# Hybrid decoder layer: one inverse form kept on TensorE and ScalarE, layer norms scaled in tile pairs

## The chip, the cores and the metric

The kernel runs on 1 core of one Trainium2 chip. The metric is device time in microseconds (us). A core has TensorE (PE: matmul; its weight loads are shown apart as PEld), VectorE (DVE), ScalarE (ACT), GpSimd (POOL) and SyncE (SP, here only DMA issues). Each runs its own list of instructions in order and waits on semaphores.

## The reference

One layer of a decoder for a prompt of 512 tokens and 8 decoding rows, width 1024. Eight heads do windowed attention, eight heads RWKV-7 time mixing; then an output projection, a layer norm, a gated convolutional FFN and a second layer norm.

```python
def layer_norm(x, g, b):
    xf = x.astype(jnp.float32)
    mu = jnp.mean(xf, -1, keepdims=True)
    xc = xf - mu
    var = jnp.mean(xc * xc, -1, keepdims=True)
    return (xc * lax.rsqrt(var + LN_EPS) * g + b).astype(x.dtype)

    # rwkv7_time_mix
    def step(S, inp):
        r_t, w_t, k_t, v_t, kk_t, a_t = inp
        sa = jnp.einsum('bhvk,bhk->bhv', S, -kk_t)
        S = S * w_t[:, :, None, :] + sa[..., None] * (kk_t * a_t)[:, :, None, :] + v_t[..., None] * k_t[:, :, None, :]
        return S, jnp.einsum('bhvk,bhk->bhv', S, r_t)

    # decoder_layer
    x1 = layer_norm(ALPHA * x + h, ln1_g, ln1_b)
    f, conv_T = conv_ffn(x1, conv_prev, w_ffn_in, conv_w, conv_b, w_ffn_out)
    y = layer_norm(ALPHA * x1 + f, ln2_g, ln2_b)
```

The recurrence over the prompt is computed in chunks of 64 tokens. For a chunk, the products of sa with each other form a unit lower triangular system, whose 64x64 inverse is needed for each head.

## The kernel before

The order of every engine is written out by hand, and semaphores count what is done. `own` behind an instruction makes an engine wait for its own result.

Stages by time: input projection with attention beside it (to about 222 us), the chunk recurrence (222 to 357), output projection with the group norm beside it (to 450), first layer norm beside the first FFN tiles (to 474), FFN (to about 836), second layer norm beside and behind the last tile of the down projection.

**The inverse.** The prompt is 4 blocks (n) of 128 tokens, each of two chunks j, held on partitions 0-63 and 64-127. `xx` holds the growing inverse X in two forms for all 8 heads: form 0 (transposed, on the other chunk's partitions) and form 1. Five levels (l = 1 to 5) double the solved size, from pairs to 64. In each level, for two groups g of 4 heads:

- `half_products` (PE): a 64x64 product of the system `lower` with form 0 for each head and chunk, into banks[4g], columns 0 to 255.
- `halves` (VectorE): that result times the mask `level[l]`, 128x256, into `lower[.., 1]`. Both groups come before any update.
- `full_products` (PE): its product with form 1 of X, in both forms, 16 products of 64x64 for a group (8 in the last level), columns 256 to 511 of banks[4g] and banks[4g+1].
- `update` (VectorE): X minus the result, both forms in one 128x512 operation; the last level makes only `xf`.

fp32 products show two matmul records each. The 64x64 products use one quarter of the array each, given by the partitions of input and output. The rest of the recurrence is laid between the levels: on PE, behind the half products of a level, the key scores (l = 1), value scores (l = 2, 3) and step terms (l = 3); in level 1 `value_side` and in level 2 `solved` are interleaved with the half products; behind the full products of level 4 come the chain product and the value terms of the block before. VectorE masks the key and value scores between `halves` and `update`, makes the transitions in level 4, and sums decode scores.

**First layer norm.** z holds 8 tiles of 128 channels, 520 tokens in two halves of 260. Per half: sums on PE, mean on VectorE, spread over partitions by a product, `ln_centre` in pairs of tiles, `ln_square` (ScalarE), sums, `ln_root` (ScalarE), `ln_recip` (VectorE), spread into bank 5. Then `ln_scale` (VectorE) multiplies tile by tile with the gain and the spread value, and `ln_shift` (ScalarE) adds the bias twice per tile: into `x1_hi`, rounded, and into z. The low part z - x1_hi is made by VectorE for pairs 0 and 2 (`even_low`), by POOL for pairs 1 and 3 (`odd_low`). PE's `ffn_half` (tile i of the FFN, one half of the tokens) waits before each k pair for its low part, for i = 0. `second_mean`, `second_var` and `second_spread` place the products of half 1's norm inside `ffn_half(0..2, 0)`, after the named k tile. `ffn_half(0, 1)` is the first that needs half 1.

**Second layer norm.** The mean of the first 7 tiles is taken off early; the last tile's down projection runs half by half. Then `l2_last`, `l2_stats`, `l2_root`, `l2_recip`, `l2_centre` (pairs), `l2_scale` (tiles) and `l2_shift` (ScalarE, the bias) lead to four stores `y_out` for each half.

## Time and profile before

| | |
|---|---|
| median of 3 runs | 873.22 us (870.77 to 873.72) |
| profiled execution | 872.92 us, span 871.1 us |
| mean granted TensorE clock | 0.984 |
| PE busy | 815.2 us, 94% |
| VectorE busy | 494.8 us, 57% |
| ScalarE busy | 330.9 us, 38% |
| POOL busy | 274.0 us, 31% |

The span goes from the first to the last instruction; the profiled execution's own time is 1.8 us longer. Times in timelines are us from the start of the span. In a timeline row stand the start, the duration (of the whole run where "xN" is over 1), engine, line, operation, output and inputs, and in brackets the idle time before it and what ended it. Many operations share the lines of helpers (L1241, L1244, L1850), so tiles tell them apart.

### The profile page before, as it was taken

The page shows a single profiled execution, that of the slowest core. Times are in us where ns is not written, and L with a number is a line of the kernel's source. Part 1 is how long each engine was busy: PE and PEld are TensorE (multiplying, and loading weights), DVE is VectorE, ACT ScalarE, POOL GpSimd, SP SyncE. Part 2 cuts the span into 40 slices and gives each one's busy share as a digit, 9 for nine tenths or more (in the row PEclk, how much of TensorE's full clock was granted, in tenths as well). Part 3 has the DMA queues.
Part 4 walks back from the last instruction along what each step waited for, and adds up shares of the span by engine and source line. Part 5 has one row for each costly group of instructions (what it writes and reads, how often), then busy time and mean ns, then how long its engine had stood idle before and what let it go on. Part 6 is the DMA issues. An engine that isn't in the chain of part 4 may idle for free.

```text
span 871.1 us, 23141 instructions
## 1 busy us (share of the span) xinstructions
PE 815.2 (94%) x10012; PEld 763.6 (88%) x10012; DVE 494.8 (57%) x764; ACT 330.9 (38%) x569; POOL 274.0 (31%) x121
## 2 busy tenths in 40 slices
PE   6999999999887777899998999999999999999994
PEld 6899889898677676688888999999999999999994
DVE  5588766786577666265354777766667661000037
ACT  5644565454313122433265434333333331111124
POOL 0000000000297670325252444444344434344300
PEclk9999999999999999999998999999999999999997
DMA  7232133152243343703111333223322332333202
GB/s 267 84 97 74 49 98 98 49 198 61 88 116 107 107 126 118 237 15 104 58 54 44 98 113 106 80 91 98 97 86 85 98 88 89 92 88 89 85 2 99
DMA packets 32470, 83.47 MB, mean 96 GB/s; under 512 B 5144, under 2 KB 10456, under 8 KB 31728
## 3 DMA queue, kind: packets, MB, share of 16 engines
q1 hardware_dynamic: 32368, 81.98, 30.7%
q8 instruction: 79, 1.29, 0.6%
q14 instruction: 23, 0.19, 0.1%
HBM read 75.87 MB, written 5.91 MB: 94 GB/s over the span
## 4 chain that ended last, share of the span: by engine, by line
PE 86%; DVE 7%; ACT 3%; issue 2%; POOL 1%; DMA 0%; DVEq 0%; ACTq 0%; POOLq 0%
PE banks L1850 83%; PE banks L1904 1%; DVE z L1241 1%; DVE xx L1241 1%; PE banks L2253 1%; DVE ms L1241 1%; DVE rw L1241 1%; DVE z L1244 1%; POOL wr_lo L697 1%; DVE ssa L1505 1%; ACT x_hi L1149 0%; ACT z L1152 0%; ACT z L1212 0%; DMA w_raw<-in_w 0%; ACT nv L982 0%
## 5 line engine op out<-in xcount | busy, mean ns | idle before, releaser
L1850 PE MATMUL banks<-x_hi,w_hi 128*128 128x264 f32 (+1 forms) x784 | 207.7, 298 | 11.4 <-DVE x_lo L1241 8.9
L1850 PE MATMUL banks<-x_hi,w_lo 128*128 128x264 f32 (+1 forms) x784 | 198.3, 286 | 0.0
L1850 PE MATMUL banks<-x_lo,w_hi 128*128 128x264 f32 (+1 forms) x784 | 198.3, 286 | 0.0
L1850 PEld LDWEIGHTS banks<-x_hi,w_hi 128*128 128x128 f32 x784 | 138.9, 191 | 24.5 <-issue 11.3
L1850 PEld LDWEIGHTS banks<-x_lo,w_hi 128*128 128x128 f32 x784 | 139.1, 192 | 0.1
L1850 PEld LDWEIGHTS banks<-x_hi,w_lo 128*128 128x128 f32 x784 | 138.9, 191 | 0.0
L697 POOL TENSOR_TENSOR w_lo<-w_raw,w_hi 128x1024 fp32r<-128x1024 f32 (+1 forms) x38 | 90.6, 2385 | 152.2 <-ACT w_hi L825 152.0
L697 POOL TENSOR_TENSOR wx_lo<-w_raw,wx_hi 128x1024 fp32r<-128x1024 f32 (+1 forms) x34 | 81.8, 2406 | 100.5 <-ACT wx_hi L825 100.1
L1244 DVE SCALAR_TENSOR_TENSOR z<-z,banks 128x260 f32<-128x260 f32 (+1 forms) x24 | 12.4, 515 | 122.1 <-PE banks L1850 121.9
L1850 PE MATMUL banks<-x_hi,wx_lo 128*128 128x260 f32 x352 | 73.5, 283 | 0.0
L1850 PE MATMUL banks<-x_hi,wx_hi 128*128 128x260 f32 x352 | 73.5, 282 | 0.0
L1850 PE MATMUL banks<-x_lo,wx_hi 128*128 128x260 f32 x352 | 73.4, 283 | 0.0
L706 POOL MEMSET kv<- 32x1536 f32 x3 | 4.1, 1373 | 220.1 <-PE banks L1850 220.0
L1850 PE MATMUL banks<-xx,lower 64*64 64x64 f32 x1280 | 54.5, 230 | 18.2 <-DVE xx L1241 13.0
L1850 PEld LDWEIGHTS banks<-xx,lower 64*64 64x64 f32 x1280 | 46.8, 140 | 26.3 <-issue 13.3
L1244 DVE SCALAR_TENSOR_TENSOR cv<-gp,par,cv 128x544 f32<-128x544 f32 x44 | 68.3, 1553 | 1.6
L1241 DVE TENSOR_TENSOR h_lo<-hh,h_hi 128x520 fp32r<-128x520 f32 x22 | 51.6, 2348 | 23.7 <-ACT h_hi L1186 23.7
L825 ACT ACTIVATE w_hi<-w_raw 128x1024 fp32r<-128x1024 f32 (+1 forms) x38 | 39.5, 1038 | 45.4 <-PE banks L1850 44.6
L1850 PEld LDWEIGHTS banks<-x_hi,wx_hi 128*128 128x128 f32 x352 | 55.4, 188 | 0.0
L1850 PEld LDWEIGHTS banks<-x_hi,wx_lo 128*128 128x128 f32 x352 | 55.4, 188 | 0.0
L1850 PEld LDWEIGHTS banks<-x_lo,wx_hi 128*128 128x128 f32 x352 | 55.2, 188 | 0.0
L825 ACT ACTIVATE wx_hi<-w_raw 128x1024 fp32r<-128x1024 f32 (+1 forms) x34 | 35.2, 1036 | 45.8 <-PE banks L1850 45.1
(254 smaller groups left out, 1713.0 us busy)
## 6 DMA issues: line engine op xcount, KB each, us to landing
w_raw<-in_w SPq DMA_DIRECT2D x87, 512.0 KB, 3.6
w_raw<-in_w SPq DMA_DIRECT2D x16, 448.0 KB, 3.3
kv<-in_ck SPq DMA_DIRECT2D x16, 192.0 KB, 4.1
kv<-in_cv SPq DMA_DIRECT2D x16, 192.0 KB, 3.4
att<-in_x SPq DMA_DIRECT2D x8, 264.0 KB, 6.0
att_out<-att SPq DMA_DIRECT2D x1, 2112.0 KB, 8.9
z<-in_xc SPq DMA_DIRECT2D x2, 1040.0 KB, 6.7
y_out<-z SPq DMA_DIRECT2D x8, 260.0 KB, 2.2
```

What stands on the lines that cost most here:

```text
L697: pool.tensor_tensor(lo[:, 0:n * P], w_raw[:, s % 2, 0:n * P], hi[:, 0:n * P].bitcast(F32), ALU.subtract)\
L706: pool.memset(kv[96:P, r * NSB * AW:(r + 1) * NSB * AW], 0.0).then_inc(kv_zero, 1)
L825: ac.activation(w_at(l)[0][:, 0:n * P], w_raw[:, s % 2, 0:n * P], ACT.Copy).then_inc(w_hi_ready, 1)
L1241: return ve.tensor_tensor(out, a0, a1, op)
L1244: return ve.scalar_tensor_tensor(out, a0, s, a1, op0, op1)
L1505: ve.tensor_reduce(ssa[:, i, :], swt[:, :, :], AX, ALU.add).then_inc(sw_y if i else sw_sa, 1)
L1850: return pe.matmul(out, l, r, start=start, stop=stop)
L1904: ins = pe.transpose(banks[:, 4 - p, j * P:(j + 1) * P], sw[:, u % 4, j * P:(j + 1) * P], ident[:, :])
L2253: ins = pe.transpose(banks[:, 6, c * P:(c + 1) * P], x[:, c, n * P:n * P + P], ident[:, :])
```

## The change

In the inverse, the masks of levels 1 to 5 change sign, so that products are added. VectorE updates form 0 only. `keep` (PE, new) multiplies form 1 by the identity into the bank, and the full products of form 1 accumulate on it; `x_copy` (ScalarE, new) copies the sum back to `xx`. This holds for levels 1 to 4; the last level stays on VectorE. In both layer norms VectorE multiplies a pair of tiles by the spread value in one operation; ScalarE applies gain and bias in its activation. In the first norm, z of pairs 1 and 3 gets gain and bias on VectorE (`odd_shift`). Some products of half 1's norm are moved to earlier k tiles, steps of the second norm are reordered on VectorE and ScalarE, and a Sqrt on one column runs ahead of its squares. Five semaphores are merged into others.

```diff
@@ -125,8 +125,9 @@
+    before, upto = k[:, None] < t[None, :], k[:, None] <= t[None, :]
+    lev[:, 1:NLEV] *= -1
     c["level"] = lev
...
@@ -961,6 +961,13 @@
+        def x_copy(n, l):
+            for g in range(2):
+                ac.wait_ge(d_ps, (NLEV - 1) * 2 * n + 2 * (l - 1) + g + 1)
+                ac.activation(xx[:, 4 * g:4 * g + 4, 1, :], banks[:, 4 * g + 1, 256:512].rearrange("p (h s) -> p h s", h=4),
+                              ACT.Copy).then_inc(xg_done, 1)
+                own(xg_done)
...
@@ -1015,17 +1022,29 @@
-        for tb in range(1, TB):
-            vt_copy(tb)
+        vt_copy(1)
+        x_copy(0, 1)
+        vt_copy(2)
+        vt_copy(3)
+        for l in range(2, NLEV - 1):
+            x_copy(0, l)
         ac.wait_ge(att_left, 16)
         for n in range(TB):
             if n >= 1:
                 b1_copy(n - 1)
+                x_copy(n, 1)
...
                 wu_copy(n - 1)
+                x_copy(n, 2)
...
+                x_copy(n, 3)
...
+                x_copy(n, 4)
                 ny_copy(n - 1)
...
@@ -1143,13 +1159,17 @@
+        def ln_high(half, c):
+
+            ac.wait_ge(ln_n, KT // 2 * half + c // 2 + 1)
+            ac.activation(x1_hi[:, c, span(half)], z[:, c, span(half)], ACT.Identity, scale=col(C_L1G + c),
+                          bias=col(C_L1B + c)).then_inc(ln_hi, 1)
+            own(ln_hi)
+
         def ln_shift(half, c):
 
-            ac.wait_ge(ln_n, KT * half + c + 1)
-            ac.activation(x1_hi[:, c, span(half)], z[:, c, span(half)], ACT.Identity, bias=col(C_L1B + c))\
-                .then_inc(ln_hi, 1)
-            own(ln_hi)
-            ac.activation(z[:, c, span(half)], z[:, c, span(half)], ACT.Identity, bias=col(C_L1B + c)).then_inc(ln_z, 1)
+            ac.activation(z[:, c, span(half)], z[:, c, span(half)], ACT.Identity, scale=col(C_L1G + c),
+                          bias=col(C_L1B + c)).then_inc(ln_z, 1)
             own(ln_z)
...
@@ -1159,7 +1179,9 @@
             for c in range(KT):
-                ln_shift(half, c)
+                ln_high(half, c)
+                if c // 2 % 2 == 0:
+                    ln_shift(half, c)
...
@@ -1208,18 +1230,18 @@
+        ac.activation(lst[:, 4, 0:1], col(C_EPS), ACT.Sqrt)
         for c in range(KT - 1):
             l2_square(c)
         l2_last(0)
         l2_root(0)
-        for c in range(5):
-            l2_shift(0, c)
         l2_last(1)
-        for c in range(5, KT):
+        for c in range(KT):
             l2_shift(0, c)
         l2_root(1)
...
@@ -1416,12 +1438,12 @@
             if l < NLEV - 1:
-                x = xx[:, hs, :, :].rearrange("p h a s -> p a h s")
-                tt(x, x, banks[:, 4 * g:4 * g + 2, 256:512].rearrange("p a (h s) -> p a h s", h=4), ALU.subtract)\
+                tt(xx[:, hs, 0, :], xx[:, hs, 0, :], banks[:, 4 * g, 256:512].rearrange("p (h s) -> p h s", h=4), ALU.add)\
                     .then_inc(d_done, 1)
             else:
+                ve.wait_ge(xg_done, 2 * (NLEV - 2) * (n + 1))
...
@@ -1682,17 +1704,26 @@
-        def ln_scale(half, c):
+        def ln_scale(half, i):
 
             ve.wait_ge(n_spread, SP_L + half + 1)
-            stt(z[:, c, span(half)], z[:, c, span(half)], col(C_L1G + c), banks[:, 5, 0:TH], ALU.mult, ALU.mult)\
-                .then_inc(ln_n, 1)
+            x = z[:, 2 * i:2 * i + 2, span(half)]
+            tt(x, x, across(5), ALU.mult).then_inc(ln_n, 1)
             own(ln_n)
 
+        def odd_shift(half, i):
+
+            ve.wait_ge(ln_hi, KT * half + 2 * i + 2)
+            for c in (2 * i, 2 * i + 1):
+                ins = ve.tensor_scalar(z[:, c, span(half)], z[:, c, span(half)], col(C_L1G + c), col(C_L1B + c),
+                                       ALU.mult, ALU.add)
+            ins.then_inc(ln_zv, 1)
+            own(ln_zv)
...
@@ -1712,29 +1743,30 @@
         ln_recip(1)
-        for c in range(KT):
-            ln_scale(1, c)
-            if c == 4:
-                even_low(1, 0)
+        ln_scale(1, 0)
+        ln_scale(1, 1)
+        ln_scale(1, 2)
+        even_low(1, 0)
+        odd_shift(1, 1)
+        ln_scale(1, 3)
         even_low(1, 2)
+        odd_shift(1, 3)
...
@@ -1830,18 +1862,18 @@
-        for c in range(5):
-            l2_scale(0, c)
+        l2_scale(0, 0)
+        l2_scale(0, 1)
         l2_last(1)
-        for c in range(5, KT):
-            l2_scale(0, c)
         l2_stats(1)
+        l2_scale(0, 2)
+        l2_scale(0, 3)
         l2_centre(1, 0)
         l2_recip(1)
         for i in range(1, KT // 2):
             l2_centre(1, i)
-        for c in range(KT):
-            l2_scale(1, c)
+        for i in range(KT // 2):
+            l2_scale(1, i)
...
@@ -2131,18 +2164,28 @@
+        def keep(n, l, g):
+
+            if l > 1:
+                pe.wait_ge(xg_done, 2 * ((NLEV - 2) * n + l - 2) + g + 1)
+            for j in range(2):
+                mm(banks[rows(j), 4 * g + 1, 256:512], level[rows(j), NLEV, :], xx[rows(j), 4 * g:4 * g + 4, 1, :], True, False)
+
         def full_products(n, l, g):
...
-                    ins = mm(banks[rows(j), 4 * g + 1, o], lower[rows(j), h, 1, :], xx[rows(j), h, 1, :])
-                    if l < NLEV - 1:
+                    ins = mm(banks[rows(j), 4 * g + 1, o], lower[rows(j), h, 1, :], xx[rows(j), h, 1, :], last, last or i == 3)
+                    if not last:
...
@@ -2278,6 +2321,9 @@
                     half_products(n, l)
+                if l < NLEV - 1:
+                    keep(n, l, 0)
+                    keep(n, l, 1)
...
@@ -2575,13 +2621,13 @@
-            if k in (2, 5):
-                ln_var(1, 2 * (k // 5))
-                ln_var(1, 2 * (k // 5) + 1)
+            if k in (1, 4):
+                ln_var(1, 2 * (k // 4))
+                ln_var(1, 2 * (k // 4) + 1)
 
         def second_spread(k):
 
-            if k == 2:
+            if k == 0:
                 ln_spread(1)
```

## Rows read from the trace of the kernel before

**Rows 1.** The page: busy time, share of the span and instructions by engine.

```profile
PE 815.2 (94%) x10012; PEld 763.6 (88%) x10012; DVE 494.8 (57%) x764; ACT 330.9 (38%) x569; POOL 274.0 (31%) x121
```

**Rows 2.** Windows over blocks 1 to 3, summed: busy us by engine.

```profile
sum 100.00, PE 76.20 PEld 67.44 DVE 63.99 ACT 29.35 POOL 56.63; mean PE 25.40 PEld 22.48 DVE 21.33 ACT 9.78 POOL 18.88
```

**Rows 3.** Windows where the clock is low: busy, then PEclk, DMA share, GB/s.

```profile
273.40:276.70 3.30, 3.30 (x126) 3.30 (x128) 2.50 (x7) 0.00 (x0) 3.22 (x2) 0.53 0.18 47
327.90:331.30 3.40, 3.40 (x69) 3.40 (x69) 0.98 (x2) 0.60 (x1) 0.00 (x0) 0.53 0.00 0
351.50:355.00 3.50, 3.50 (x52) 3.05 (x50) 2.11 (x7) 3.18 (x4) 1.78 (x1) 0.51 1.05 309
471.10:477.90 6.80, 5.41 (x25) 5.11 (x25) 1.78 (x5) 2.54 (x4) 2.06 (x2) 0.50 0.00 0
```

**Rows 4.** Groups by form (count, busy us, mean ns); then an ACT timeline row.

```profile
L1241 DVE TENSOR_TENSOR xx<-xx,banks 128x512 f32<-128x512 f32 x32 | 22.0, 687 | 4.5 <-PE banks L1850 3.5
L1241 DVE TENSOR_TENSOR lower<-banks,level 128x256 f32<-128x256 f32 x40 | 17.0, 425 | 25.8 <-PE banks L1850 24.0 <-DVE lower L1241 0.4
L1290 DVE TENSOR_SCALAR sw<-sw,rinv 128x256 f32<-128x256 f32 x8 | 2.8, 353 | 0.3
...
280.15 0.80 ACT L987 ACTIVATE yy<-banks 128x256 f32<-128x256 f32 x2
```

**Rows 5.** Timeline of PE at the start of an inverse: start us, duration us.

```profile
252.68 0.66 PE L1850 MATMUL banks<-level 64*64 64x256 f32 x8
253.17 0.22 PE L1850 MATMUL banks<-level,lower 64*64 64x64 f32 x1
```

**Rows 6.** Timeline of DVE, block 0, levels 2 and 3.

```profile
238.29 1.41 DVE L1241 TENSOR_TENSOR xx<-xx,banks 128x512 f32<-128x512 f32 x2 [2.21 <-PE banks L1850]
239.83 0.43 DVE L1241 TENSOR_TENSOR lower<-banks,level 128x256 f32<-128x256 f32 x1
241.14 1.41 DVE L1241 TENSOR_TENSOR xx<-xx,banks 128x512 f32<-128x512 f32 x2 [0.17 <-PE banks L1850]
```

**Rows 7.** Timelines: DVE in block 1, level 3; PE in block 2, level 4.

```profile
268.67 0.42 DVE L1241 TENSOR_TENSOR ms<-banks,causal 128x256 f32<-128x256 f32 x1 [0.97 <-PE banks L1850]
...
308.07 0.59 PE L1850 MATMUL banks<-carry,mt 64*64 64x64 f32 x13 [1.22 <-DVE rw L1241]
```

**Rows 8.** Timelines of four engines, first layer norm, half 1.

```profile
449.83 0.70 DVE L1241 TENSOR_TENSOR x_lo<-z,x_hi 128x520 fp32r<-128x520 f32 x1
452.65 0.93 DVE L1241 TENSOR_TENSOR x_lo<-z,x_hi 128x520 fp32r<-128x520 f32 x1
...
461.63 1.00 PE L1850 MATMUL banks<-lst,lsel 128*128 128x65 f32 x8
...
462.74 2.56 DVE L1244 SCALAR_TENSOR_TENSOR z<-z,par,banks 128x260 f32<-128x260 f32 x5 [1.87 <-PE banks L1850]
...
463.31 0.51 ACT L1149 ACTIVATE x_hi<-z,par 128x260 fp32r<-128x260 f32 x1 [3.10 <-DVE z L1244]
...
472.17 1.28 POOL L767 TENSOR_TENSOR x_lo<-z,x_hi 128x520 fp32r<-128x520 f32 x1 [3.07 <-ACT z L1152]
...
473.51 0.59 PE L1850 MATMUL banks<-x_hi,w_hi 128*128 128x260 f32 x1 [1.39 <-POOL x_lo L767]
```

**Rows 9.** Timelines of ACT, PE and DVE, second layer norm.

```profile
848.72 1.28 ACT L1206 ACT_TABLE_LOAD   x1 [6.21 <-DVE lst L1244]
...
855.21 0.28 PE L1850 MATMUL banks<-h_hi,wx_lo 128*128 128x260 f32 x1
...
856.59 0.42 DVE L1241 TENSOR_TENSOR z<-z,banks 128x260 f32<-128x260 f32 x1
858.61 0.22 DVE L1801 TENSOR_SCALAR lst<-banks 128x65 f32<-128x65 f32 x1
...
859.45 0.35 ACT L1206 ACTIVATE lst<-lst,par 128x65 f32<-128x65 f32 x1
864.20 4.32 ACT L1212 ACTIVATE z<-z,par 128x260 f32<-128x260 f32 x8 [4.40 <-DVE z L1244]
```

More of the change, by code:

```diff
@@ L684, in _ @@
             for c in range(0, KT, 2):
-                sp.wait_ge(ln_z, 2 * KT + KT * half + c + 2)
+                sp.wait_ge(ln_z, KT + KT * half + c + 2)
                 sp.dma_start(a["y_out"][:, c:c + 2, span(half)], z[:, c:c + 2, span(half)]).then_inc(outs, 16)
@@ L764, in odd_low @@
             pool.wait_ge(ln_hi, KT * half + 2 * i + 2)
-            pool.wait_ge(ln_z, KT * half + 2 * i + 2)
+            pool.wait_ge(ln_zv, 2 * half + i // 2 + 1)
             x = slice(2 * i, 2 * i + 2)
@@ L1028, in _ @@
                 wu_copy(n - 1)
+                x_copy(n, 2)
+                if n == TB - 1:
+                    ac.wait_ge(s_pback, 1)
+                    ac.activation(sprob[:, :, :], banks[:, 7, 0:NSB * B * H].rearrange("p (t n) -> p t n", t=NSB),
+                                  ACT.Copy).then_inc(s_prob, 1)
+                    own(s_prob)
+                x_copy(n, 3)
                 if n == 1:
@@ L1209, in l2_shift @@
         def l2_shift(half, c):
-            ac.wait_ge(ln_n, 2 * KT + KT * half + c + 1)
-            ac.activation(z[:, c, span(half)], z[:, c, span(half)], ACT.Identity, bias=col(C_L2B + c)).then_inc(ln_z, 1)
+            ac.wait_ge(ln_n, KT + KT // 2 * half + c // 2 + 1)
+            ac.activation(z[:, c, span(half)], z[:, c, span(half)], ACT.Identity, scale=col(C_L2G + c),
+                          bias=col(C_L2B + c)).then_inc(ln_z, 1)
             own(ln_z)
+        ac.activation(lst[:, 4, 0:1], col(C_EPS), ACT.Sqrt)
         for c in range(KT - 1):
@@ L1819, in l2_recip, with l2_scale @@
             own(n_inv)
-        def l2_scale(half, c):
+        def l2_scale(half, i):
             ve.wait_ge(n_spread, SP_M + half + 1)
-            stt(z[:, c, span(half)], z[:, c, span(half)], col(C_L2G + c), banks[:, (5, 7)[half], 0:TH],
-                ALU.mult, ALU.mult).then_inc(ln_n, 1)
+            x = z[:, 2 * i:2 * i + 2, span(half)]
+            tt(x, x, across((5, 7)[half]), ALU.mult).then_inc(ln_n, 1)
             own(ln_n)
@@ L2137, in full_products @@
             pe.wait_ge(p_done, k + 1)
-            if l == NLEV - 1 and n + 1 < TB:
+            last = l == NLEV - 1
+            if last:
+                pe.wait_ge(xg_done, 2 * (NLEV - 2) * n + 2 * (NLEV - 2) - 1 + g)
+            if last and n + 1 < TB:
                 pe.wait_ge(sc_ps, 2 * n + g + 3)
```

57 lines of the change are left out of this document (25 added, 32 removed).

## The prediction

> **What bounds the kernel now.** I read first the page's busy shares: TensorE (PE) is busy 94% of an 871.1 us span, VectorE 57%, ScalarE 38% [rows 1]. So a saving on VectorE or ScalarE counts only where PE waits for them. The second view is the windows over the chunk recurrence, which the first half of the change touches: in its three later blocks PE is busy 76.2 of 100 us, VectorE 64.0, ScalarE 29.4 [rows 2]. About 24 us of PE idle lie there, and that is the prize. The third view is the timeline around both layer norms, since there PE stands still for ScalarE, VectorE and GpSimd (POOL), and after the last large product, from 855.21 to 855.49, a tail of 15.6 us follows [rows 9]. The fourth is the clock: four stretches of 3.3, 3.4, 3.5 and 6.8 us show 0.50 to 0.53, the lower level (1.2 GHz), and each begins after PE had been waiting [rows 3].
>
> **Part A, the inverse: the prices.** There are 4 blocks with 5 levels each. In levels 1 to 4 VectorE updated both forms, 128x512 in 0.687 us, once for each of two groups of heads; now it updates one form, 128x256. The nearest row, the masks of the same shape from the same place, takes 0.425 [rows 4]. With the gap between instructions that is 0.28 less per group: group 0 is ready 0.28 earlier and group 1 0.56 earlier in a level. ScalarE gets 32 copies of 128x256; two such copies from PSUM take 0.80 us [rows 4], 0.40 each, some 13 us on an engine that is busy less than a third of this stage. No PE step waits for a copy that would come late: the form is next read a whole half product later. Hence nothing for ScalarE; were that cover gone, 0.40 per level.
>
> PE gets 4 products with a 64x64 identity and 256 columns per level (two groups, two diagonal quarters of the array). The row for it is in the start of the inverse: four of these products, one in each quarter, let the next one start 0.49 us after the first (252.68 to 253.17) [rows 5]. Two on the diagonal cost the same as four, so a level costs two rounds one after the other, 0.86 to 0.98; I take 0.86, since the first round's rows overlap the half products, which use the other two quarters. The bounds are 0, if it all fits beside them, and 0.98. The 16 levels make 13.8 us of PE. The minus sign in the masks and the add instead of the subtract cost nothing.
>
> The Trainium skill (TensorEngine Tiling (Array Packing), Key Properties) says that different tiles of the array can load and multiply in parallel. The row of four products in 0.49 us agrees with this. By that rule alone the identity products would be free beside the half products, which is the first rival below.
>
> **Part A, where it falls.** The identity products are issued after the half products of both groups and ahead of everything else of the level. But PE's idle time lies before the half products, where it waits for the update, not behind them: in block 0, level 3, the half product of group 1 waits for the update that ends at 239.70, and the full products must start when the mask of 239.83 is done at 240.26 [rows 6]. About 0.1 us is free there, not 0.86. So the level that was 2.85 us long (238.29 to 241.14 [rows 6]) gains 0.28 and 0.56 at its updates and loses about as much again. Followed through block 0: the full products are 0.86 late in level 1, 0.86 in level 2, 0.92 in level 3; level 4 starts behind two bonus products on PE, where the earlier update brings nothing, and adds 0.22: 1.14 us.
>
> In the later blocks the work that follows on PE feeds VectorE. Level 1: key scores 0.86 later, so their masks, so the update; its own gain leaves the half products of level 2 some 0.50 late. Level 2: those are interleaved with the solved products, PE-bound, then 0.86 more before the value scores; their mask had no slack, the update is 1.30 late, and less 0.28 level 3 begins 1.02 late. Level 3: the half product of group 1 is 0.28 closer, the identity products add 0.86, so step terms and value scores are 0.60 later still; the mask that waited 0.97 us for them [rows 7] and the update behind it are 1.62 late. Level 4: the half product of group 1 is 1.06 late, the transitions on VectorE too, and the chain product, which waited 1.22 us for them in block 2 [rows 7], hides this level's identity products. That makes 1.06 us for blocks 2 and 3 each and, with no chain step in block 1, 0.90 there. Sum of part A at one clock: 1.14 + 0.90 + 1.06 + 1.06 = +4.2 us. Queued behind PE's new waits for the copies are the full products; I cost those waits at nothing, as above.
>
> The clock gives some back. The stretch from 327.9 follows waits in block 3, level 1, which the new products partly fill. The three low stretches in this stage make the work in them about 1.5, 0.7 and 1.5 us longer (half of what they hold, as far as PE bounded it): 3.7 at most. I take 1.4, and 0 and 3.7 as ends. Part A: +2.8.
>
> **Part B, first layer norm.** PE stands at 473.51 for the last low part of half 1 [rows 8]. That chain: spread at 461.63, scale on VectorE from 462.74, then 16 ScalarE steps of 0.51 (0.545 with the gap) from 463.31, then POOL from 472.17 for 1.28. New: the statistics products move one k tile earlier, but the second must wait for its square (a 0.3 us stall), so the spread, moved two tiles (0.72) ahead, comes 0.43 earlier. A pair scale takes 0.70 where one tile took 0.49, so ScalarE starts 0.21 earlier. It then has 12 steps, not 16: the last high part ends at 463.10 + 12 x 0.545 = 469.6. VectorE adds two affine steps of 128x260; the nearest row, 128x256 with a scalar per partition, is 0.353 [rows 4], so 0.41 each at most. 470.5 + 0.13 + 1.28 = 471.9, and PE goes on at about 471.97: -1.55 us. Bounds: -0.8 (the affine steps at 0.7 each) and -2.1. What is late next is the even low part of the third pair, 469.3, before it. Behind 473.51 PE ran at the lower clock to 477.9 [rows 3], which costs half of 4.4 us, 2.2. PE now waits about 2.1 us instead of 3.1 just ahead of this; the dip may go or stay. I take half, -1.1, with ends 0 and -2.2. Half 0 is hidden behind rwkv_out products.
>
> VectorE's even low part took 0.93 us at 452.65 beside POOL, 0.70 elsewhere in the same shape [rows 8]. The Trainium skill (VectorE: DVE Perf Modes, The perf-mode tier table) gives a single-input fp32 step from SBUF twice the rate; the Trainium skill's GPSIMD Engine Reference (Specifications) says that POOL shares its SBUF interfaces with VectorE, with contention in such a mode or with two SBUF inputs. That agrees with the slower low part. By that, the odd affine steps would slow POOL or be slowed. In this order POOL waits while they run, so I add nothing; the row's 0.23 would be the price.
>
> **Part B, second layer norm.** The 1.28 us table load at 848.72 [rows 9] leaves the path, but the centring waits for the spread mean, so only some 0.7 us come of it, and half 1's last product ends at 855.5 in any case. VectorE then takes it at 855.6 instead of 856.59, behind five scales [rows 9]. Statistics of half 1 come at 857.0 instead of 858.61. But ScalarE now squares first and does all 8 shifts of half 0 after it: 856.5 + 8 x 0.545 = 860.9. The root of half 1 is queued behind these and runs at 860.9, not 859.45. Reciprocal, three centrings (2.2 us) and a pair scale lead to 864.9 for the first shift, which was at 864.20 [rows 9]. The 8 shifts and the store follow as before: +0.7 us (0 to +1.2). Unused semaphores merged: nothing, as their transfers land tens of us ahead.
>
> **Sum.** 4.2 - 1.4 - 1.55 - 1.1 + 0.7 = +0.85 us. Against the profiled execution, 872.92, that is 873.8; against the median, 873.22, it is 874.1. I say 874.0.
>
> **Rivals.** (1) The identity products hide beside the half products. Then each level brings its 0.28: -0.9 in block 0, -1.4 in the others, -5.1; with part B (-1.95) some 866 us. For it: separate quarters, 24 us of idle. Against: order of issue, and idle on the wrong side. 0.18. (2) The clock pays nothing back: the same lost 0.86 per level, decided by the dips staying in place after each wait. 4.2 - 1.55 + 0.7 = +3.35, 876.6; with identity products at 0.98 and a new dip, 880. 0.30. (3) The order does not do what it says: the layer norm gains nothing since ScalarE's steps with both scale and bias last longer than 0.51. No row has such a step; at 0.6 it is +1.1 us for half 1 and +0.7 at the end, 875.8. 0.07. (4) All dips of the stage go: 4.2 - 3.7 - 1.55 - 2.2 + 0.7 = -2.55, 870.7. 0.10. The forecast has 0.35.
>
> **How the numbers follow.** About 0.3%, 2.6 us, is what a measurement can tell from no change. Faster by more: rival 1 and half of 4, 0.23. Slower by more: rival 2, part of 3 and of the forecast's upper side, 0.34. Same: 0.43. The range runs from 868.0, inside rival 1, to 879.0.
>
> **What would show it.** Right: about 32 ScalarE copies of 0.40; PE busy more than 10 us longer between 222 and 360, and that stage 2 to 4 us longer; updates of 0.42; PE's wait for the last POOL part ending 1 to 2 us earlier after the spread; ScalarE's second root directly behind eight shifts. Wrong: the stage is shorter, with full products starting directly behind the masks; or the low-clock stretches gone. A first shift of half 1 less than 9.0 us after the last large product's end (8.7 before, 9.4 forecast) would refute the tail.

## The result, and the profile after

| | median us | runs |
|---|---|---|
| kernel before | 873.47 | 4 |
| changed kernel | 881.32 (880.79 to 882.75) | 4 |

The ratio is 1.0112, 95% interval 1.0087 to 1.0136. That is 9.8 us slower by the ratio and 7.9 by the two medians. The forecast was 874.0 us, its range ended at 879.0. The profiled execution has a span of 881.0 us, 9.9 more than the one of before; it was the slowest of its four, so one or two of these 9.9 us are scatter.

The page's busy line of the changed kernel, answering [rows 1], and the window over blocks 1 to 3 (columns: busy us of PE, PEld, DVE, ACT, POOL, then granted clock, DMA share, GB/s), answering [rows 2]:

```profile
PE 826.3 (94%) x10140; PEld 772.7 (88%) x10140; DVE 486.8 (55%) x756; ACT 342.8 (39%) x594; POOL 274.2 (31%) x121
```

```profile
257.00:357.00 100.00, 80.76 (x2790) 70.64 (x2790) 55.83 (x117) 39.14 (x88) 54.80 (x18) 0.95 0.40 118
```

PE is busy 11.1 us more, ScalarE 11.9 more, VectorE 8.0 less. In the window PE has 4.6 us more, VectorE 8.2 less, ScalarE 9.8 more. The work moved as the diff says; what VectorE gave up was not what PE had to wait for.

Groups of VectorE and ScalarE by form in the changed kernel (count, busy us, mean ns), answering [rows 4] and [rows 8]:

```profile
L1263 DVE TENSOR_TENSOR xx<-xx,banks 128x256 f32<-128x256 f32 x32 | 13.5, 420 | 6.5 <-PE banks L1882 5.5
...
L967 ACT ACTIVATE xx<-banks 128x256 f32<-128x256 f32 x32 | 12.3, 384 | 39.2 <-PE banks L1882 37.9
L1165 ACT ACTIVATE x_hi<-z,par 128x260 fp32r<-128x260 f32 x16 | 9.7, 605 | 6.1 <-DVE z L1263 5.7
L1171 ACT ACTIVATE z<-z,par 128x260 f32<-128x260 f32 x8 | 4.8, 605 | 0.3
L1234 ACT ACTIVATE z<-z,par 128x260 f32<-128x260 f32 x16 | 9.6, 603 | 4.2 <-DVE z L1263 3.7
```

The 32 copies are there, 0.38 us each. All 40 affine steps of ScalarE take 0.60 us, where those with a bias alone took 0.51 [rows 8].

VectorE in block 0, levels 2 and 3 (timeline: start us, duration us), answering [rows 6]:

```profile
238.35 0.89 DVE L1263 TENSOR_TENSOR xx<-xx,banks 128x256 f32<-128x256 f32 x2 [2.90 <-PE banks L1882]
241.28 0.89 DVE L1263 TENSOR_TENSOR xx<-xx,banks 128x256 f32<-128x256 f32 x2 [0.77 <-PE banks L1882]
```

A level takes 2.93 us where it took 2.85 [rows 6], although its updates are 0.27 shorter each (0.42 in place of 0.69).

The first layer norm, four engines, answering [rows 8]:

```profile
456.86 2.84 DVE L1263 TENSOR_TENSOR x_lo<-z,x_hi 128x520 fp32r<-128x520 f32 x1
...
456.75 2.39 POOL L697 TENSOR_TENSOR wx_lo<-w_raw,wx_hi 128x1024 fp32r<-128x1024 f32 x1
...
459.75 0.59 PE L1882 MATMUL banks<-x_hi,w_hi 128*128 128x260 f32 x1 [2.37 <-DVE x_lo L1263]
...
471.66 0.60 ACT L1165 ACTIVATE x_hi<-z,par 128x260 fp32r<-128x260 f32 x1 [2.94 <-DVE z L1263]
...
480.30 1.28 POOL L767 TENSOR_TENSOR x_lo<-z,x_hi 128x520 fp32r<-128x520 f32 x1 [2.54 <-DVE z L1718]
...
481.63 0.39 PE L1882 MATMUL banks<-x_hi,w_hi 128*128 128x260 f32 x1 [1.76 <-POOL x_lo L767]
```

VectorE's low part of the third pair runs beside GpSimd's weight low parts and takes 2.84 us (0.93 before). PE, which needs it, stands idle for 2.37 us. Half 1 ends with PE going on at 481.63, 8.1 us after the 473.51 of before; the inverse had brought only 4.2 of that.

The second layer norm, the last large product and ScalarE behind it, answering [rows 9]:

```profile
862.80 0.28 PE L1882 MATMUL banks<-h_hi,wx_lo 128*128 128x260 f32 x1
...
864.16 5.06 ACT L1234 ACTIVATE z<-z,par 128x260 f32<-128x260 f32 x8
869.25 0.35 ACT L1228 ACTIVATE lst<-lst,par 128x65 f32<-128x65 f32 x1
873.28 5.05 ACT L1234 ACTIVATE z<-z,par 128x260 f32<-128x260 f32 x8 [3.68 <-DVE z L1263]
```

From that product's end, 863.08, to the first shift of half 1 it is 10.2 us (8.7 before, 9.4 forecast), and the last shift ends 15.3 after it (13.0 before).

Stretches of the changed kernel with a low granted clock (last three columns: granted clock, DMA share, GB/s), answering [rows 3]:

```profile
274.00:280.00 6.00, 5.51 (x198) 4.95 (x202) 4.22 (x10) 4.09 (x7) 5.27 (x2) 0.72 0.07 22
328.00:334.00 6.00, 4.63 (x101) 4.26 (x95) 2.76 (x6) 2.28 (x5) 0.00 (x0) 0.72 0.11 33
351.00:356.00 5.00, 2.25 (x28) 2.14 (x29) 0.89 (x3) 4.86 (x6) 0.54 (x1) 0.72 1.01 268
356.00:361.00 5.00, 5.00 (x87) 4.53 (x85) 2.84 (x11) 0.98 (x2) 4.25 (x2) 0.59 1.05 338
456.00:464.00 8.00, 5.63 (x49) 5.33 (x50) 4.52 (x5) 1.17 (x3) 5.82 (x3) 0.69 0.31 104
482.00:490.00 8.00, 8.00 (x57) 8.00 (x56) 4.76 (x6) 3.22 (x4) 2.40 (x1) 0.79 0.20 66
```

None of the dips of [rows 3] (stretches at the lower level of the clock) went in this execution. The two last in this list are one behind PE's wait at 459.75, which is new, and the one behind 481.63.

So the 9.9 us of the two traces are: 0.8 us less up to the inverse, 5.0 more in it, 3.9 more in the first norm up to 481.63, 0.5 less in the products that follow (482 to 863), 2.2 more in the tail, and 0.1 in what remains.

### The profile page after: what moved, and what is told of

Same layout as the page of the kernel before. It is cut to its first block, busy times and chain, and to the rows that moved or that the text cites. A ratio compares the mean times of both kernels' runs of the same rounds, so it can differ in the third digit from the quotient of the medians.

```text
span 881.0 us, 23441 instructions
## 1 busy us (share of the span) xinstructions
PE 826.3 (94%) x10140; PEld 772.7 (88%) x10140; DVE 486.8 (55%) x756; ACT 342.8 (39%) x594; POOL 274.2 (31%) x121
## 3 DMA queue, kind: packets, MB, share of 16 engines
q8 instruction: 80, 1.31, 0.6%
## 4 chain that ended last, share of the span: by engine, by line
PE 87%; DVE 6%; ACT 3%; issue 2%; POOL 1%; DMA 0%; DVEq 0%; ACTq 0%; POOLq 0%
PE banks L1882 85%; ACT z L1234 1%; PE banks L1936 1%; PE banks L2296 1%; DVE ms L1263 1%; DVE z L1263 1%; DVE rw L1263 1%; ACT x_hi L1165 1%; POOL wr_lo L697 1%; DVE xx L1263 1%; DVE ssa L1527 1%; DMA w_raw<-in_w 0%; DVE x_lo L1263 0%; DVE sscore L1496 0%; DVE gyc L1263 0%
## 5 line engine op out<-in xcount | busy, mean ns | idle before, releaser
L1266 DVE SCALAR_TENSOR_TENSOR cv<-gp,par,cv 128x544 f32<-128x544 f32 x44 | 70.4, 1599 | 1.6
```

The lines of the kernel that those rows point to most:

```text
L1266: return ve.scalar_tensor_tensor(out, a0, s, a1, op0, op1)
```

## The experiments

Three lengths and a clock are read from the trace of every kernel. *Stage* is from the start of the last low part of the attention mix to VectorE's first sum of the attention output. *Norm 1* is from the reciprocal of half 0 to the end of PE's last wait for a low part of half 1. *Tail* is from the end of the last large product to the end of the last affine step. *Clock* is the mean granted clock from 450 to 500 us, the end of the first norm and what follows it. e5 and e9 leave out a part of the arithmetic and keep the order of the work.

| kernel | ratio to before (95%) | stage | norm 1 | tail | clock |
|---|---|---|---|---|---|
| before | 1 | 139.9 | 33.6 | 13.0 | 0.93 |
| changed | 1.0112 (1.0087 to 1.0136) | 144.9 | 37.5 | 15.3 | 0.90 |
| e1 inverse alone | 1.0058 (1.0030 to 1.0087) | 145.3 | 33.6 | 13.5 | 0.97 |
| e2 norm 1 alone | 1.0033 (1.0012 to 1.0053) | 138.2 | 35.1 | 13.1 | 0.97 |
| e3 norm 2 alone | 1.0029 (1.0011 to 1.0047) | 141.0 | 33.6 | 15.3 | 1.00 |
| e4 GpSimd waits | 1.0060 (1.0037 to 1.0083) | 148.7 | 32.9 | 15.3 | 1.00 |
| e5 no identity products | 1.0046 (1.0024 to 1.0068) | 141.5 | 36.4 | 15.3 | 0.93 |
| e6 identity products twice | 1.0268 (1.0237 to 1.0299) | 158.7 | 37.5 | 15.3 | 0.90 |
| e7 identity products behind | 1.0076 (1.0049 to 1.0104) | 142.8 | 37.8 | 15.3 | 0.93 |
| e8 root first | 1.0077 (1.0048 to 1.0107) | 143.6 | 37.6 | 13.2 | 0.90 |
| e9 other operands | one run | 143.9 | 32.9 | 15.3 | 1.00 |
| e10 changed, again | 1.0106 (1.0080 to 1.0132) | 143.1 | 36.2 | 15.3 | 0.97 |
| e11 mended | 0.9947 (0.9927 to 0.9968) | 139.7 | 30.7 | 11.7 | 1.00 |
| e12 mended, new inverse | 1.0002 (0.9983 to 1.0022) | 146.1 | 30.7 | 11.7 | 1.00 |
| e13 load later | 0.9993 (0.9976 to 1.0011) | 141.5 | 33.6 | 13.0 | 0.93 |
| e14 mended, load later | 0.9935 (0.9910 to 0.9960) | 139.1 | 30.7 | 11.7 | 1.00 |

The six traces with the old inverse have stages of 138.2 to 141.5, mean 139.9; the seven with the changed one (changed, e1, e4, e8, e9, e10, e12) 143.1 to 148.7, mean 145.1. One trace alone tells the stage to 2 or 3 us, and the tail to half a us (13.5 in e1, whose second norm is that of before, with 13.0).

**Each part alone.** e1 takes the two layer norms of before, e2 and e3 the inverse of before and one of the norms; the merged semaphores stay in all three.

> Only the change to the inverse (one form added up on TensorE with the identity products, copied back by ScalarE) is made to the kernel before. Theory S (the inverse costs what the trace after shows, about 5.0 us up to the attention step at 366, and the clock gives nothing back): 873.5 + 5.0 = 878.5 us. Theory F (as forecast, the clock pays part back): +2.8, 876.3 us. Theory N (the inverse costs little, and what stands late at 366 came from somewhere else in the combined kernel): within 1 us of 873.5.

> Only the first layer norm is changed (pairs on VectorE, gain and bias on ScalarE, odd parts on VectorE, spread moved ahead). Theory C (collision): ScalarE's shorter list ends early, so GpSimd's two weight steps start early and VectorE's even low part of the third pair runs beside them for 2.8 us instead of 0.93; the half 1 chain is about 3 to 4 us later: 876.5 to 877.5 us. Theory I (the collision came only since the inverse was late and will not show alone): ScalarE's 12 steps of 0.64 against 16 of 0.545 give about 1 us less, 872.5 us, and the low part stays under 1.0 us.

> Only the second layer norm is changed. Theory T (tail as the trace after shows: 8 shifts of 0.63 ahead of the second root, then 8 shifts of 0.63): from the end of the last large product to the end of the span 17.9 us instead of 15.6, so +2.3: 875.8 us. As forecast: +0.7, 874.2 us.

Measured: 877.0, 874.7 and 874.9 us beside 872.5. The three excesses, 0.58, 0.33 and 0.29%, add up to 1.20%, and the whole gave 1.12 and, measured again (e10), 1.06%: no part gains. e1's interval holds theory S, and by its low end F too; its stage is 5.4 us over that of before. e3 has theory T's tail to the tenth. In e2 the collision of theory C is there without the new inverse:

VectorE's low part of the third pair in e2:

```profile
452.22 2.82 DVE L1245 TENSOR_TENSOR x_lo<-z,x_hi 128x520 fp32r<-128x520 f32 x1
```

Rival I falls. But the price of C was too high: norm 1 is 1.5 us longer, not 3 to 4. The other 2.4 us of the changed kernel's 3.9 are a dip of the clock behind the collision: the granted clock between 456 and 464 is 0.69 in the changed kernel and 1.00 in e2. e10, the same program as the changed kernel, had 0.79 there, and 36.2 us; it had no dip at 274 and none behind the last wait of the norm.

**The collision taken away (e4).**

```diff
+        pool.wait_ge(ln_lo_even, 2)
         w_low(10)
         w_low(11)
```

> The changed kernel, with one wait more on GpSimd: its two weight low parts between the halves of the first layer norm start only after VectorE's even low part of the third pair. Theory C (both engines' steps on SBUF collide): that low part takes 0.70 instead of 2.84 us, TensorE's 2.4 us gap at 459.75 shrinks below 1 us, and the kernel is 2 to 4 us faster than the changed one, 877.3 to 879.3 us. Rival R (ScalarE's longer steps set the end of half 1 in any case): the low part may be short, yet the total stays within 1 us of 881.3.

VectorE's low part and GpSimd's weight low parts in e4:

```profile
460.36 0.70 DVE L1264 TENSOR_TENSOR x_lo<-z,x_hi 128x520 fp32r<-128x520 f32 x1
...
461.19 2.42 POOL L697 TENSOR_TENSOR wx_lo<-w_raw,wx_hi 128x1024 fp32r<-128x1024 f32 x1 [1.03 <-DVE x_lo L1264]
```

The low part takes 0.70, norm 1 falls from 37.5 to 32.9, and the ratio from 1.0112 to 1.0060, although this execution's stage was the longest of all, 148.7. Theory C stands. The clock has a share in it: e4 has no dip in the norm (1.00 from 450 to 500, where the changed kernel has 0.90), and the 4.6 us by which norm 1 is shorter are some 2.1 of the collision (e2 has 35.1, e4 32.9) and the dip behind it. The trace of before had the collision already, in the feed-forward part. A low part of the same shape beside a weight low part of GpSimd, in the kernel before, and the page's group of all 22:

```profile
485.07 2.36 DVE L1241 TENSOR_TENSOR h_lo<-hh,h_hi 128x520 fp32r<-128x520 f32 x1 [1.08 <-ACT h_hi L1186]
...
484.44 2.44 POOL L697 TENSOR_TENSOR w_lo<-w_raw,w_hi 128x1024 fp32r<-128x1024 f32 x1 [4.89 <-ACT w_hi L825]
...
L1241 DVE TENSOR_TENSOR h_lo<-hh,h_hi 128x520 fp32r<-128x520 f32 x22 | 51.6, 2348 | 23.7 <-ACT h_hi L1186 23.7
```

GpSimd's step ends at 486.88, VectorE's 0.55 us later: VectorE's step, begun second, is held about until GpSimd's is done. All 22 of these steps end 0.55 or 0.56 us behind GpSimd's, and so does the step of 0.93 in [rows 8], which began 0.38 us before the end (453.03) of a GpSimd step of 1.31 us. So 0.23 was no price of the collision, only what was left of that step. The Trainium skill's GPSIMD Engine Reference (Specifications), on the SBUF interfaces that the two share, agrees with these rows. The forecast had cited it and then named 0.23 as its price.

**The identity products (e5, e6, e7).** e5 leaves them out; e6 issues each twice; e7 puts them behind the full products and releases VectorE before them:

```diff
-                if l < NLEV - 1:
-                    keep(n, l, 0)
-                    keep(n, l, 1)
...
                     full_products(n, l, 0)
                     full_products(n, l, 1)
+                    keep(n, l, 0)
+                    keep(n, l, 1)
```

> The changed kernel without the identity products (the first form is left out of the sum, so the inverse is another number; everything else runs as before). Theory P (PE's two rounds per level lie on the path, 0.86 a level): the stage from the last part of the attention mix to the first sum of the attention output, 144.9 us in the changed kernel and 139.9 before, falls by 0.86 in about 12 of 16 levels, 8 to 10 us, and the kernel by as much, to about 872 us. Rival H (they fit beside the half products and the late updates come from ScalarE's copies): the stage changes by less than 2 us, the kernel stays above 879 us.

> The changed kernel with each identity product issued twice, the second over the first. Theory P (on the path): 0.86 more in 16 levels less what the waits of block 0 and the chain products hide, 8 to 13 us, so 889 to 894 us. Rival H (beside other work): under 2 us more, 883 us at most.

> The changed kernel with the identity products moved behind the full products of their level, where PE waits for VectorE's update; VectorE is released before them, ScalarE's copy after them. Theory P (the order of issue was the fault, since PE's idle time lies ahead of the half products): most of the 0.86 a level is hidden, the stage falls by 5 to 9 us to 136 to 140 us, the kernel to 873 to 876 us. Rival Q (the later copy then becomes the last thing that the next full products wait for, 0.86 + 0.40 behind the full products): the stage stays within 2 us of 144.9, the kernel at 880 us.

Doubling adds 13.8 us to the stage, and 13.9 by the ratios (1.0268 against 1.0109, the mean of both measurements): 16 levels by 0.86 is 13.76. So the price of a level was right, and so was that PE's path carries a second set in full (rival H falls). Leaving the first set out gives back 3.4 us by the trace and 5.5 by the ratios (1.0046), where 8 to 10 were expected. By blocks: block 0, from the stage's start to VectorE's last update in it, takes 32.00 us, 0.85 less than the 32.85 of e3, which has the inverse of before and the same low clock at 222; the forecast for free identity products was -0.9. Blocks 1 and 2 together (from VectorE's last update of the inverse in block 0 to that in block 2) take 65.7, 0.9 more than the 64.7 of before. There e5 has this PE wait (timeline) and these windows (granted clock third from the end):

```profile
266.36 0.45 PE L1882 MATMUL banks<-rw,aa 64*64 64x64 f32 x9 [2.88 <-issue]
...
266.00:271.00 5.00, 4.33 (x150) 4.14 (x153) 2.93 (x6) 0.77 (x2) 4.84 (x3) 0.66 0.45 137
276.00:281.00 5.00, 4.87 (x208) 4.73 (x207) 3.38 (x8) 1.25 (x3) 3.54 (x2) 0.66 0.02 3
```

A stall of 2.88 us on "issue" and two dips to 0.66 stand where the gain should be. With the shorter updates and no identity products at all, the stage of e5 (141.5) is still not under that of before (139.9): by this trace the shorter updates gained 0.9 us in block 0 and nothing in the three later ones. e7 lies nearer to rival Q than to theory P: 2.1 us off the stage, and 3 us by the ratios, whose intervals overlap. The waits of PE for VectorE's updates, 1.2 and 1.1 us in blocks 1 and 2 of the changed kernel, are 0.4 us and less in it, but other idle time takes their place. PE's waits in the stage by what ended them (total us, times, longest), in the kernel before and then in e7:

```profile
PE banks L1850 <- DVE xx L1241: 13.0, 11, 2.7
PE banks L1850 <- issue: 7.3, 7, 2.7
```

```profile
PE banks L1883 <- issue: 13.1, 11, 3.7
PE banks L1883 <- DVE xx L1264: 1.2, 4, 0.4
```

The waits for the updates fall by 11.8 us and those on "issue" rise by 5.8; e5 has 11.9 on "issue", the changed kernel 7.9. So a wait taken from PE's path in this stage is only in part a gain.

**The second root (e8).** In ScalarE's list the second root stands behind two shifts of half 0:

```diff
-        for c in range(KT):
+        for c in range(2):
             l2_shift(0, c)
         l2_root(1)
+        for c in range(2, KT):
+            l2_shift(0, c)
```

> The changed kernel with ScalarE's root of half 1 of the second layer norm behind two shifts of half 0 and not behind eight. Theory T (the eight shifts of 0.63 hold the root, 3.9 us after its input is there): root at 2.3 us after the end of the last large product instead of 6.2, and the end of the span 14.3 us after that product instead of 17.9; 877.8 us. Rival V (VectorE's centring and scaling of half 1 are late anyway): less than 1 us gained, 880.5 us or more.

The root and the eight shifts of half 1 in e8, whose last large product ends at 862.92:

```profile
865.30 0.35 ACT L1228 ACTIVATE lst<-lst,par 128x65 f32<-128x65 f32 x1
871.01 5.06 ACT L1234 ACTIVATE z<-z,par 128x260 f32<-128x260 f32 x8 [1.54 <-DVE z L1265]
```

The root comes 2.4 us after the product, not 6.2; the tail is 13.2 us, 2.1 less and back at that of before. Theory T has the root right and the gain too large. It expected 3.6 us; behind the root, centring and scaling take 5.7 us in place of 4.0. The ratio, 1.0077, is 3 us under that of the changed kernel, with intervals that overlap; it is the tail that shows the gain.

**What makes an affine step 0.60 (e9).**

> The changed kernel with other operands in ScalarE's steps of the first layer norm, all 128x260: high parts of half 0 with a gain per partition and no bias, of half 1 with a fixed gain of 1.25 and a bias per partition; shifts of z of half 0 plain copies, of half 1 a fixed gain alone (so the norm's gain and bias are partly left out). Theory O (each operand read per partition adds 0.09 us to a step of 0.42): 0.51, 0.51, 0.42 and 0.42 us. Theory G (a gain per partition is what makes it 0.60, since the steps with a bias alone took 0.51): 0.60, 0.51, and at most 0.51 for both copies. Theory K (the kind of function sets it, not the operands): all of one function alike.

Groups of ScalarE in e9: high parts of half 0 and 1, then z of half 1 and 0:

```profile
L1169 ACT ACTIVATE x_hi<-z,par 128x260 fp32r<-128x260 f32 x8 | 4.1, 513 | 3.7 <-DVE z L1269 3.5
L1166 ACT ACTIVATE x_hi<-z,par 128x260 fp32r<-128x260 f32 x8 | 4.1, 513 | 3.1 <-DVE z L1269 2.9
L1176 ACT ACTIVATE z<-z 128x260 f32<-128x260 f32 x4 | 1.7, 422 | 0.1
L1178 ACT ACTIVATE z<-z 128x260 f32<-128x260 f32 x4 | 1.7, 421 | 0.1
```

L1166 and L1169 are the two forms of the high part, L1176 and L1178 those of z. A gain per partition alone gives 0.51, a bias alone 0.51, neither 0.42, a fixed gain 0.42: theory O. The kind of function does not set it: Copy is among those of 0.51 and those of 0.42. An operand read per partition adds 0.09 us to a step of 128x260, and a second one adds it again.

**A mended kernel (e10, e11, e12).** e11 has the inverse of before, e4's wait, e8's order, and gives VectorE work that ScalarE had on the path; in the second norm VectorE also does the affine steps of the odd pairs of half 1:

```diff
         for i in range(KT // 2):
+            ln_scale(1, i)
+        odd_shift(1, 0)
+        even_low(1, 0)
+        for i in range(1, KT // 2):
+            odd_shift(1, i)
+        even_low(1, 2)
+        even_low(1, 3)
...
-        for c in range(KT):
+        for c in (0, 1, 4, 5):
             l2_shift(1, c)
```

> The changed kernel once more, unaltered, beside the next two on the same chip. If the first measurement stands: 1.009 to 1.014 of the kernel before. If it was partly the chance of few runs, whose parts alone added up to 1.012 (1.0058, 1.0033, 1.0029): down to 1.006.

> The inverse as before, both layer norms changed and mended: GpSimd's weight steps wait for VectorE's low part; in half 1 of the first norm VectorE does all shifts of z and the low parts of pairs 2 and 3, ScalarE the eight high parts alone; in the second norm the root of half 1 stands behind two shifts, and VectorE shifts the odd pairs of half 1. Theory M (each part costs what the traces showed): first norm 0.7 for the collision's absence and 2.5 from 8 high parts of 0.64 in place of 12 steps, less what TensorE's two waits of 0.9 and 1.8 don't hold; second norm 0.9 ahead of the last product and 3.1 behind it: 5 to 7 us under the kernel before, 866 to 868 us, ratio 0.992 to 0.994. Rival W (VectorE's shifts beside GpSimd's low part are held as its low part was, and turn into the new wait): the first norm gains nothing, 869 to 870 us.

> The last kernel with the changed inverse put back in. Theory P (the identity products are on TensorE's path, whatever the norms do): 4.5 to 6 us slower than the mended kernel, ratio to it 1.005 to 1.007. Rival C (part of the inverse's price is the clock's dip at the norms, which the mended norms no longer have): under 3 us slower.

e10 confirms the first measurement. e11 is 868.1 us beside 873.5, 0.53% under the kernel before (0.32 to 0.73%), just short of theory M's 0.992 to 0.994, into which the interval reaches. Its rows in norm 1 and in the tail:

```profile
466.28 0.70 DVE L1250 TENSOR_TENSOR x_lo<-z,x_hi 128x520 fp32r<-128x520 f32 x1
467.01 3.27 DVE L1705 TENSOR_SCALAR z<-z,par 128x260 f32<-128x260 f32 x6
...
467.92 1.43 POOL L768 TENSOR_TENSOR x_lo<-z,x_hi 128x520 fp32r<-128x520 f32 x1 [9.00 <-ACT x_hi L1150]
...
471.07 0.39 PE L1876 MATMUL banks<-x_hi,w_hi 128*128 128x260 f32 x1 [0.67 <-DVE x_lo L1250]
...
854.47 0.35 ACT L1213 ACTIVATE lst<-lst,par 128x65 f32<-128x65 f32 x1
...
863.09 0.74 DVE L1867 TENSOR_SCALAR z<-z,par 128x260 f32<-128x260 f32 x2
```

VectorE's low part keeps its 0.70 and the tail is 1.3 us shorter than before, norm 1 3.0. Rival W is true in part. Six affine steps from 467.01 on take 3.27 us where six of 0.37 are 2.2, and GpSimd's low part, which runs beside them, 1.43 in place of 1.29. One of the six is held: it begins at 468.12, 0.20 us behind GpSimd's step, takes 1.39 and ends 0.14 behind it. That is about 1.1 us on the path to 471.07, and part of why the gain is short of M. So the hold takes affine steps with one tensor input too. The two pages that the prediction named agree with that (the Trainium skill, VectorE: DVE Perf Modes, The perf-mode tier table; GPSIMD Engine Reference, Specifications). The forecast had excluded it by the order of the work, and in the changed kernel that order did hold. e12 puts the changed inverse back: 872.1 us, and 0.55% over e11, some 4.8 us (4.0 by the medians). That is theory P, though the scatter of the runs reaches down to rival C's 3 us. The price of the inverse is about the same with the mended norms as with those of before (0.58% in e1).

The mended norms also have the better clock. All seven kernels in which VectorE's low part takes 2.8 us and PE waits 2.3 to 2.4 us for it have dips between 450 and 500; of the four with the norm of before (before, e1, e3, e13) three have; the four in which that low part takes 0.70 (e4, e11, e12, e14) have none there, nor has e9, where it takes 2.15. Over all their runs the mean granted clock is 0.986 to 0.989 in these four, 0.982 and 0.983 in the two measurements of the changed kernel and 0.983 to 0.985 in the kernel before.

**What holds the stage (e13, e14).** PE's longest idle of the stage, 2.71 us at 348.22 in the kernel before, ends on "issue". The load of half of the residual input was issued later:

```diff
-        sp.wait_ge(bt_ps, 3 * TB - 2)
-        sp.dma_start(z[:, 0:CC, :], a["xc"][:, 0:CC, :]).then_inc(z_landed, 16)
         values_of(2)
         values_of(3)
         sp.wait_ge(bt_ps, 3 * TB - 1)
+        sp.dma_start(z[:, 0:CC, :], a["xc"][:, 0:CC, :]).then_inc(z_landed, 16)
```

> The kernel before; only the load of the first half of the residual input (1040 KB), which is issued at 341.98, stands behind two value loads and goes together with the second half at about 353. Theory D (PE's idle of 2.71 us at 348.22, which ends on nothing that the profile shows, is an instruction packet that has to pass the data packets of a DMA share of 1.0): the idle falls to 1.1 to 1.5 us, as the one of 1.45 us at 310.34 with almost no data traffic, and the stretch up to 361.85 with it; 1 to 1.5 us less, 872 us. Rival E (it ends on something else, such as ScalarE's steps at 346.85 to 351.96): 2 to 3 us as before, no change in time. If the later load makes the attention sums wait, they start after 363.

> The mended kernel (inverse as before) with the same move of the load. Theory D: 1 to 1.5 us less than the mended kernel, ratio to the kernel before 0.993. Rival E: 0.9947 again.

Two idles of PE in the kernel before, then that of e13, first its row and then its window:

```profile
310.34:311.80 1.46, 0.01 (x3) 0.00 (x1) 0.00 (x0) 0.00 (x0) 1.46 (x1) 1.00 0.00 0
348.22:350.93 2.71, 0.00 (x0) 0.00 (x0) 0.00 (x0) 2.62 (x7) 0.00 (x0) 1.00 1.02 265
```

```profile
351.94 0.91 PE L1849 MATMUL banks<-xx,lower 64*64 64x64 f32 x22 [2.33 <-issue]
...
349.61:351.94 2.33, 0.00 (x1) 0.00 (x1) 0.00 (x0) 2.25 (x6) 0.00 (x0) 1.00 0.87 219
```

The idle in e13 is 2.33 us and the time is unchanged (0.9993, 0.9976 to 1.0011). The edit did not take the traffic away, since the value loads moved up into its place and the DMA share is 0.87; so it decides neither theory. Against the traffic stands the idle at 310.34: 1.46 us with a DMA share of 0.00. e14 (0.9935) can't be told from e11. In the six kernels with the old inverse this idle is 2.1 to 2.9 us (mean 2.4), in the ten whose inverse is changed in any way 2.7 to 3.8 (mean 3.4). That 1.0 us is part of the inverse's price.

What ends these idles can be read from the DMA packets in the traces. The page of before has a queue of instruction packets (packets, MB, share), of which this one goes with PE: its 79 packets stand beside 20024 records of PE and PEld, some 253 for each, and the changed kernel, with 256 records more, has 80.

```profile
q8 instruction: 79, 1.29, 0.6%
```

The sixteen traces have 63 idles of PE on "issue" of over 0.9 us between 215 and 372. Every one of them ends 1.2 to 1.8 us (mean 1.4) after the end of the last packet of this queue before it. The idle at 310.34 ends 1.56 us behind a packet that ended at 310.24; the one at 348.22 ends 1.43 us behind a packet that went from 348.39 to 349.50. Of moments chosen at random in this stretch 12% lie so. So these idles are most likely waits of PE for its next instructions. That is read from the order of events and not shown by an experiment: no run here changed how the instructions are brought, and why the wait of block 3 is longer with the changed inverse stays open.

## Why the prediction was wrong, by its own steps

**Part A.** The terms were right in kind: 0.86 a level (e6: 13.8 for 16), updates 0.27 shorter (0.42 against 0.69), and no wait of PE or VectorE in any trace ends on one of ScalarE's copies. +4.2 were forecast at one clock; +5.2 is the difference of the means, clock included. The time that a stage spent at the lower level follows from its mean granted clock: 3.4 to 13.7 us with the old inverse (mean 9.7) and 6.8 to 17.1 with the changed one (mean 11.2). Traces with as much low time differ by 4 to 5 us: with 6.8 us of it 138.2 against 143.1 and 143.9, with 10.2 us 139.9 and 139.7 against 145.3 and 143.6, with 13.7 us 141.0 and 141.5 against 144.9 and 146.1. So at one clock it is about +4.7.

By place the sizes differ. As means of the six and the seven traces, block 0 costs 1.7 us (1.14 forecast), blocks 1 and 2 together 0.4 (1.96), block 3 2.9 (1.06). Of the two signs for the stage, 2 to 4 us longer was exceeded, and PE busy more than 10 us longer between 222 and 360 came out at 5.8 (116.3 against 110.5); over the whole stage, which is 5 us longer, it is 10.0. The forecast's gain for free identity products, 5.1 us, is not borne out either (e5). In block 3 of the changed trace (2.6 us longer) 0.7 us are the longer idle on "issue":

```profile
353.75 1.55 PE L1882 MATMUL banks<-xx,lower 64*64 64x64 f32 x24 [3.40 <-issue]
```

It was 2.71 before. The step that failed is "The clock gives some back": in place of -1.4, the changed inverse had 1.5 us more of low time on average, a cost of about half a us. Rival 2 had that with +4.2, and it was given 0.30 and the forecast 0.35. The reasoning took a dip for a debt that the filling of a wait pays off. The traces of one program show that dips come and go between executions. The kernel before and e3 have the same program from 474 to 490, and here is that stretch in the one and in the other:

```profile
474.00:490.00 16.00, 16.00 (x121) 16.00 (x121) 10.32 (x11) 7.17 (x9) 7.63 (x3) 0.88 0.21 67
```

```profile
474.00:490.00 16.00, 16.00 (x136) 16.00 (x135) 11.06 (x13) 7.16 (x9) 7.62 (x3) 1.00 0.24 67
```

0.88 and 1.00: x121 and x136 matmuls in the same 16 us. One trace can't give such a term its size, and in the stage filling a wait earned nothing. An edit can earn one even so: the four kernels without PE's wait of 2.4 us in the first norm have no dip there.

**First layer norm.** Three terms. The end of ScalarE's list: forecast -1.55 for the end of half 1. From reciprocal 1 to PE's going on it is 12.8 us against 13.2, -0.4. The term mis-sized is the affine step: 12 steps of 0.60 plus gap make 7.6 us, not 6.5, that is +1.1. This is rival 3 with its very number, given 0.07. PE's wait for the last GpSimd part was to end 1 to 2 us earlier after the spread; counted from the spread's products (461.63 before, 469.76 in the changed kernel) it ended after 11.9 us in both, and the 0.4 us are the spread that comes sooner after the reciprocal. The rows to foresee it were in the trace of before: a square of 128x260 without operand takes 0.42 and the shift with a bias 0.51 [rows 8], 0.09 for one operand. The group of that square in the kernel before:

```profile
L1200 ACT ACTIVATE zsq<-z 128x260 f32<-128x260 f32 x2 | 0.8, 420 | 0.6 <-DVE z L1241 0.5
```

The second term was left out: what else the shorter list sets free. In half 0, GpSimd's low part of the last pair ends 12.57 us after the reciprocal of half 0, where it was 13.15, and in both kernels GpSimd's weight step follows directly on it; the high part that this step reads was ready in both. VectorE's low part of the third pair came at the same place as before, 12.8 us after that reciprocal. So GpSimd's weight step moved from 0.45 us behind that part's start to 0.11 us ahead of it. The prediction said "POOL waits while they run, so I add nothing" of the affine steps, and did not follow GpSimd's next instructions: +1.5 alone (e2), and about 0.7 of gain without it (e4: 32.9 against 33.6). The third term, -1.1 for a dip that might go, became a dip more: +2.4 behind the collision in the changed trace, 1.1 in e10, 0 in e2.

**Second layer norm.** Forecast +0.7, measured +2.2 in the tail. The order of events was right, with the root behind eight shifts. Nearly all of the miss (1.4 of 1.5 us) is the 0.09 a step: 8 shifts ahead of the root 0.7, 8 shifts of half 1 another 0.7. The first shift of half 1 at 10.2 us was to refute the tail only if under 9.0; the mechanism stood. Rival 3 priced these two rows of shifts at 0.7 together; they were twice that.

**The sum.** With the sizes of the trace after: inverse +5.0, norm 1 -0.4 + 1.8 + 2.4, tail +2.2, products between them -0.5, start -0.8: 9.7 of the 9.9 us. The three parts alone add to 10.5 (1.20%). The forecast had subtracted 1.4 + 1.1 for the clock, priced the affine steps 2.5 too low (1.1 in the first norm, 1.4 in the second), and left out the collision.

**The rivals.** Rival 1 (identity products hidden) is refuted by e6, and its gain by e5. Rival 4 (all dips go) by the rows of the clock. Rivals 2 and 3 were both true, and nothing excluded that. They were priced as alternatives to each other, at 876.6 and 875.8; both together are 878.4, and the collision's 1.5 us bring that past the range's end at 879.0.

## What to carry to other kernels

Price a step by a row with the same operands, not only the same shape: on ScalarE each operand per partition was 0.09 us on 128x260, and 28 such steps on the path cost 2.5 us more than forecast. When a list of one engine gets shorter, follow it to the engine that it feeds and to what stands next in that engine's own list, and look for what will run beside it; then look in the whole trace for the same pair of forms side by side. Give a granted clock that recovers no credit from one trace; compare several executions with the wait and without it.

## What was not expected of the hardware

- A two-input step of VectorE on SBUF (128x520) beside one of GpSimd (128x1024) took 2.8 us in place of 0.70 in seven executions, and 22 more in the kernel before took 2.35 on average; each ended 0.55 us behind GpSimd's step. Affine steps of 0.37 beside GpSimd's 128x520 lost about 1.1 us between them in e11.
- ScalarE, 128x260: 0.42 us with no operand per partition, 0.51 with a gain or a bias, 0.60 with both.
- PE stood still on "issue" for 1.0 to 3.8 us two to six times in the stage of every execution, once with no data traffic at all, and each time until 1.2 to 1.8 us after an instruction packet had ended.
- The stage with the same inverse took 143.1 to 148.7 us in seven kernels, and 144.9 and 143.1 in two executions of one program.
